# Attention probabilities in a one-core Trainium2 kernel: split into f16 halves in SBUF and turned by transposing transfers

## The chip, the core and the metric

The kernel runs on one core of a Trainium2 chip. The core has five engines that run on their own and meet at semaphores: TensorE (PE, matmuls into PSUM), VectorE (DVE), ScalarE (ACT), GpSimd (POOL, which works in SBUF here) and SyncE (SP, which issues nearly all transfers). Sixteen DMA engines move data between HBM and SBUF and inside SBUF. The metric is the device time of one execution in microseconds.

## What is computed

A block with two branches, a gated delta rule and a sparse latent attention, merged by gates and projected. Only the attention matters here. With T = 1024 tokens, 8 heads, a latent of rank 256, and for each query at most 256 chosen keys:

```python
logits = jnp.einsum('bqhc,bqkc->bqhk', ql, kv).astype(f32)
bias = rel_bias[t5_bucket(t[None, :, None] - sel)]
logits = logits + jnp.moveaxis(bias, -1, 2).astype(f32)
logits = jnp.where(valid[:, :, None, :], logits, -jnp.inf)
p = jax.nn.softmax(logits, axis=-1).astype(kv.dtype)
return jnp.einsum('bqhk,bqkc->bqhc', p, kv)
...
ob = jnp.einsum('bthc,chd->bthd', o_lat, w_uv[l]).reshape(B, T, DSA_W) * jax.nn.silu(zb)
```

The kernel builds keys and values of each head from the latent, computes the logits against all earlier keys, and adds a mask that closes the keys that were not chosen. Its f32 matmuls are three f16 ones: each operand is split into a high half and a low half (the rest), and `three` (L92) adds high x high, high x low and low x high.

## The kernel before

The program has a front (projections and choice of keys), a delta-rule stage, the attention (`phase_attention`, L2325) and a merge (`phase_merge`, L2122). The order on each engine is the order of its code; nothing is scheduled.

The attention walks over 64 steps n = (h, i), eight query tiles i of 128 tokens for each head h, in the order 0, 7, 1, 6, 2, 5, 3, 4 (`ORDER`). A step is `wide[n]` = 128 (i + 1) columns wide, so a head has 36 blocks of 128x128, and narrow and wide steps alternate: 128, 1024, 256, 896, 384, 768, 512, 640. Work on one step is spread over loops that run at different distances:

- PE, loop pass n: logits of step n (L2427), transposes of step n - 3 from SBUF into PSUM (`turn`, L2442), products with the values of step n - 5 (`values`, L2455), and in every second pass a piece of the next head's keys or values (`piece`, L2397).
- ACT, pass n: exp of step n - 1 with its row sums (`soften`, L2495), the high half of a piece (L2486), the high half of the turned probabilities of step n - 3 from PSUM (`split_p`, L2500), the high half of the gated output of step n - 7 (`split_b`, L2508).
- DVE, pass n: reciprocal of the row sums of step n - 2 (`norm`, L2553), logits plus mask with the row extreme for step n - 1 (`peak`, L2542, which reads PSUM and `added`), gate of step n - 6 (`gate`, L2566), low half of the turned probabilities of step n - 4 (`split_p`, L2559), low half of a piece (L2531).
- POOL, pass n: scaling of the probabilities of step n - 2 by the reciprocal (L2614), low half of the gated output of step n - 8 (L2619), mask plus bias for step n + 2 (`near`, L2599). In eight passes it also splits a part of the output weights (L2627).
- SP loads one gate row block of 512 KB per head (L2389).

Probabilities lie in four places of `g.o` (`place`); wide scores have one place in PSUM (banks 0 and 1) and narrow ones another, and the turned blocks use banks 3 to 5. Scores of step n wait until `peak` of step n - 2 is done. In each pass DVE's reciprocal waits for ACT's exp of the same step, ACT's exp for DVE's peak, and DVE's low half of a piece for ACT's high half of it.

## Time and profile before

| | |
|---|---|
| time, median of 3 runs | 1411.44 us (1408.17, 1411.44, 1420.66) |
| span of the profiled execution | 1410.0 us |
| PE busy in the span | 1375.1 us (98%) |
| DVE, ACT, POOL busy | 923.7 us (66%), 716.5 us (51%), 599.8 us (43%) |
| attention stage | about 1063 to 1237 us from the span's start |

The profile is one execution, recorded by the hardware profiler. A timeline row gives the start (us from the span's start), the duration in us, the engine, the line of the kernel, the operation and its tiles as out<-in with partitions x elements; in brackets stands how long the engine sat idle before it and what released it. Instructions on one engine overlap at their ends, so the next one can start a little before the listed end. A group row gives the count, busy us, the mean duration in ns, and idle time with its releaser. Ends of matmuls are modelled; starts are read.

### The profile page before, as it was taken

The numbers are of one execution on the slowest core, as the hardware profiler recorded it, in microseconds if no ns is written. First come the engines' busy times: TensorE is split into PE (matmuls) and PEld (weight loads), VectorE is DVE, ScalarE is ACT, GpSimd is POOL, SyncE is SP. The second block draws the span as 40 slices with busy tenths as digits, with TensorE's granted clock in tenths as the row PEclk, the third lists the DMA queues.
The fourth block names the chain that finished last, engine by engine and source line by source line (L and its number), as shares of the span: only waits on it lengthen the run. The fifth ranks groups of instructions, "written<-read, shape, count | busy, mean of one in ns | idle before, by whom it ended". The sixth has DMA issues, their size and how long they took to land.

```text
span 1410.0 us, 27056 instructions
## 1 busy us (share of the span) xinstructions
PE 1375.1 (98%) x10290; PEld 843.0 (60%) x10298; DVE 923.7 (66%) x1958; ACT 716.5 (51%) x1525; POOL 599.8 (43%) x717
## 2 busy tenths in 40 slices
PE   6999999999999999999999999999999999999997
PEld 6555994444444556666666666554446878844444
DVE  4879887777334577678778775446716777747344
ACT  4758777785433554655665663333215777701111
POOL 0074677778752442541531530003104777764000
PEclk9989999999999999999999999999999999999999
DMA  9401333333323321322222222337652000085122
GB/s 366 140 8 31 93 106 113 120 121 110 108 90 124 84 71 52 87 63 72 82 66 67 83 71 80 122 97 276 199 197 103 31 22 26 17 305 157 38 97 90
DMA packets 137642, 147.50 MB, mean 105 GB/s; under 512 B 16706, under 2 KB 109738, under 8 KB 135852
## 3 DMA queue, kind: packets, MB, share of 16 engines
q1 hardware_dynamic: 136668, 141.31, 31.8%
q10 hardware_dynamic: 720, 4.46, 0.8%
q8 instruction: 81, 1.33, 0.4%
q14 instruction: 45, 0.37, 0.1%
q0 software_dynamic: 128, 0.03, 0.0%
HBM read 114.40 MB, written 31.15 MB: 103 GB/s over the span
## 4 chain that ended last, share of the span: by engine, by line
PE 58%; DVE 3%; POOL 2%; issue 2%; DMA 2%; ACT 2%; SPq 1%; DVEq 0%; POOLq 0%; ACTq 0%
PE ps L94 15%; PE ps L96 15%; PE ps L95 15%; PE ps L2451 2%; DVE g_yq L1632 1%; POOL g_shared L1397 1%; PE ps L1915 1%; PE ps L2039 1%; POOL g_shared L1399 1%; PE ps L2023 1%; PE ps L2022 1%; PE ps L2018 1%; PE ps L2038 1%; PE ps L1953 1%; DMA g_shared<-diagonal_blocks 1%
## 5 line engine op out<-in xcount | busy, mean ns | idle before, releaser
L94 PE MATMUL ps<-g_h_hi,g_piece_hi 128*128 128x512 f16 x544 | 206.9, 380 | 1.6 <-PEq L2662 1.6
L95 PE MATMUL ps<-g_h_lo,g_piece_hi 128*128 128x512 f16 x544 | 206.3, 379 | 0.0
L96 PE MATMUL ps<-g_h_hi,g_piece_lo 128*128 128x512 f16 x544 | 206.2, 379 | 0.0
L1397 POOL TENSOR_TENSOR g_shared<-g_shared 128x120 f32<-128x120 f32 (+14 forms) x120 | 58.0, 483 | 181.7 <-DMA g_shared<-diagonal_blocks 171.3
L1010 DVE TENSOR_SCALAR_CACHE_REDUCE a_ada<-a_ada,a_s_all 128x896 bf16<-128x896 f32 (+1 forms) x124 | 113.0, 967 | 1.0
L1632 DVE SCALAR_TENSOR_TENSOR g_yq<-e_raw,g_taps,g_yq 128x1024 f32<-128x1024 f32 x60 | 92.3, 1539 | 21.5 <-ACT g_yq L1461 19.7
L94 PE MATMUL ps<-g_o,g_h_hi 128*128 128x128 f16 (+2 forms) x424 | 101.4, 266 | 1.7 <-DVE l_b L2572 1.6
L96 PE MATMUL ps<-g_o,g_h_lo 128*128 128x128 f16 (+2 forms) x424 | 101.4, 266 | 0.4
L95 PE MATMUL ps<-g_o,g_h_hi 128*128 128x128 f16 (+2 forms) x416 | 98.3, 264 | 0.0
L96 PEld LDWEIGHTS ps<-g_h_hi,g_piece_lo 128*128 128x128 bf16 x544 | 53.3, 98 | 64.4 <-issue 0.3
L94 PEld LDWEIGHTS ps<-g_h_hi,g_piece_hi 128*128 128x128 f16 x544 | 53.3, 98 | 53.4 <-issue 2.2
L95 PEld LDWEIGHTS ps<-g_h_lo,g_piece_hi 128*128 128x128 f16 x544 | 53.3, 98 | 50.2
L2614 POOL TENSOR_SCALAR g_o<-g_o,l_share 128x128 f32<-128x128 f32 (+3 forms) x64 | 47.9, 748 | 72.3 <-DVE l_share L2557 71.9
L1493 ACT ACTIVATE g_shared<-ps,e_s_neg 128x128 f32<-128x128 f32 x56 | 20.6, 368 | 104.5 <-PE ps L2023 104.2
L1623 DVE TENSOR_TENSOR g_piece_lo<-g_piece,g_piece_hi 128x1024 bf16<-128x1024 f32 x40 | 50.0, 1250 | 30.9 <-ACT g_piece_hi L1544 30.8
L310 POOL TENSOR_TENSOR a_work<-a_w,a_work 128x512 bf16<-128x512 f32 x48 | 56.6, 1195 | 15.3 <-ACT a_work L722 15.3
L310 POOL TENSOR_TENSOR a_parts<-a_w,a_parts 128x512 bf16<-128x512 f32 x48 | 55.1, 1165 | 13.3 <-ACT a_parts L722 13.3
L2497 ACT ACTIVATE g_o<-g_o,l_top 128x128 f32<-128x128 f32 (+3 forms) x64 | 49.7, 776 | 20.6 <-DVE l_top L2550 18.7
L739 ACT ACTIVATE a_ada<-a_ada,a_s_all 128x1024 bf16<-128x1024 f32 (+1 forms) x62 | 57.3, 927 | 0.7 <-DVEq L1032 0.7
L1399 POOL TENSOR_TENSOR g_shared<-g_shared 128x120 f32<-128x120 f32 (+14 forms) x120 | 53.6, 447 | 9.4
L2506 ACT CAST g_o<-ps 128x128 f16<-128x128 f32 (+3 forms) x64 | 40.7, 636 | 26.5 <-PE ps L2451 24.9
L1544 ACT CAST g_piece_hi<-g_piece 128x1024 f16<-128x1024 f32 x40 | 41.6, 1040 | 24.0 <-DMA g_piece<-in_w_o_gdn 22.4
(437 smaller groups left out, 4052.1 us busy)
## 6 DMA issues: line engine op xcount, KB each, us to landing
a_w<-in_w_in SPq DMA_DIRECT2D x17, 1024.0 KB, 5.8
g_piece<-in_w_in SPq DMA_DIRECT2D x34, 512.0 KB, 4.1
channel_gates<-a_ada SPq DMA_DIRECT2D x48, 256.0 KB, 2.2
g_shared<-diagonal_blocks SPq DMA_DIRECT2D x32, 256.0 KB
a_ada<-in_w_ada ACTq DMA_DIRECT2D x4, 1024.0 KB, 9.5
a_x<-in_x SPq DMA_DIRECT2D x8, 512.0 KB, 8.9
delta_gate<-a_ada SPq DMA_DIRECT2D x16, 256.0 KB, 2.5
g_shared<-sums_by_head SPq DMA_DIRECT2D x8, 512.0 KB, 4.3
```

Source lines behind the costliest of these rows:

```text
L94: pe.matmul(out, a_hi, b_hi, start=first, stop=False)
L95: pe.matmul(out, a_hi, b_lo, start=False, stop=False)
L96: return pe.matmul(out, a_lo, b_hi, start=False, stop=last)
L310: nc.gpsimd.tensor_tensor(op_lo[v % 2][:, x], of, op_hi[v % 2][:, x], ALU.subtract).then_inc(w_ready, 1)
L739: nc.scalar.activation(mask[:, g.first[i]:g.first[i + 1]], score[:, g.first[i]:g.first[i + 1]], ACT.Sign, bias=trial[:, 4 + e:5 + e], accu ...
L1010: mark(("count", e), nc.vector.tensor_scalar(spent_of(i), rows_of(i), trial[:, e:e + 1], offset[:, e:e + 1], ALU.is_ge, ALU.add, accum_out ...
L1397: nc.gpsimd.tensor_tensor(part, table[:, j, :, j + 1:BASE], tc[:, :, j:j + 1].broadcast_to([P, NT, left]), ALU.mult).then_inc(sub, 1)
L1399: last = nc.gpsimd.tensor_tensor(tc[:, :, j + 1:BASE], tc[:, :, j + 1:BASE], part, ALU.subtract)
L1623: nc.vector.tensor_tensor(w_lo[:, m % 3], w32[:], w_hi[:, m % 3], ALU.subtract).then_inc(w_ready, 1)
L1632: nc.vector.scalar_tensor_tensor(out=y, in0=raw[:, m % 2, PAD - 3 + j:PAD - 3 + j + T], scalar=g.taps[:, tap:tap + 1], in1=y, op0=ALU.mult ...
L2497: nc.scalar.activation(p(n), p(n), ACT.Exp, scale=-1.0, bias=top[:, n % 4:n % 4 + 1], accum_out=total[:, n % 4:n % 4 + 1]).then_inc(exp_ok, 1)
L2614: nc.gpsimd.tensor_scalar(p(m), p(m), share[:, m % 4:m % 4 + 1], 1.0, ALU.mult, ALU.mult).then_inc(shared, 1)
```

## The change

Five things change in `phase_attention`:

- The transposes on PE, their PSUM banks and the two reads of them (ACT's high half, DVE's low half) are gone. ACT makes the high half straight from the probabilities in SBUF, multiplied by the reciprocal, as f16 (`high`); DVE computes probability x reciprocal - high half with one SCALAR_TENSOR_TENSOR (`low`). Both halves of a step lie side by side in one of four staging buffers, in tiles that the earlier stages used.
- SP issues one transposing transfer a step, SBUF to SBUF, of both halves (2 x `wide[n]` columns). It waits for both halves and, from step 4 on, for the products of step n - 4. `high` of step n waits for the transfer of step n - 4.
- POOL's scaling is gone. POOL takes over the high half of the gated output from ACT, ahead of its low half.
- Wide scores get a second place (bank 3), so their logits wait for the peak of step n - 4. Outputs alternate between banks 5 and 6.
- The distances: `high` and `low` stand in the pass of the reciprocal (n - 2), products at n - 6, gate at n - 7.

```diff
+        staged = lambda n: (rest[:, 2 * T:], wide_a, narrow_b, rest)[n % 4][:, 0:2 * wide[n]]
...
-            return (0 if steps[n][1] >= 4 else 2) * BANK
+            return ((0, 3)[n // 2 % 2] if steps[n][1] >= 4 else 2) * BANK
...
+            for n in range(N):
+                sp.wait_ge(high_ok, n + 1)
+                sp.wait_ge(low_ok, n + 1)
+                if n >= 4:
+                    sp.wait_ge(pv, n - 3)
+                sp.dma_start_transpose(pt(n), staged(n)).then_inc(turned[n % 4], 16)
+                h = n // 8 + 1
+                if n % 8 == 5 and 2 <= h < H:
                     sp.wait_ge(got, NT * (h - 1))
-                sp.dma_start(z[:, h % 2], g.sig_dram[h * P:(h + 1) * P, :]).then_inc(z_in[h % 2], 16)
+                    sp.dma_start(z[:, h % 2], g.sig_dram[h * P:(h + 1) * P, :]).then_inc(z_in[h % 2], 16)
...
-                if n >= 2:
+                if steps[n][1] < 4 and n >= 2:
                     pe.wait_ge(top_ok, n - 1)
-                pe.wait_ge(kv_l, 4 * h + 2)
+                elif n >= 4:
+                    pe.wait_ge(top_ok, n - 3)
+                pe.wait_ge(kv_l, 4 if n == 3 else 4 * h + 2)
...
             def values(n):
                 h, i = steps[n]
-                pe.wait_ge(pt_l, n + 1)
+                pe.wait_ge(turned[n % 4], TURNED_BEFORE + 16 * (n // 4 + 1))
...
+            def high(n):
+                act.wait_ge(inv, n + 1)
                 if n >= 4:
+                    act.wait_ge(turned[n % 4], TURNED_BEFORE + 16 * (n // 4))
+                nc.scalar.activation(staged(n)[:, 0:wide[n]], p(n), ACT.Copy, scale=share[:, n % 4:n % 4 + 1]).then_inc(high_ok, 1)
...
+                if 0 <= n - 2 < N:
+                    high(n - 2)
                 if 0 <= n - 1 < N:
                     soften(n - 1)
                 if piece_of(n - 1) is not None and n != 4:
                     piece(piece_of(n - 1))
-                if 0 <= n - 3 < N:
-                    split_p(n - 3)
-                if 0 <= n - 7 < N:
-                    split_b(n - 7)
...
+            def low(n):
+                dve.wait_ge(high_ok, n + 1)
+                nc.vector.scalar_tensor_tensor(out=staged(n)[:, wide[n]:], in0=p(n), scalar=share[:, n % 4:n % 4 + 1], in1=staged(n)[:, 0:wide[n]],
+                                               op0=ALU.mult, op1=ALU.subtract).then_inc(low_ok, 1)
...
-                if 0 <= n - 6 < N:
-                    gate(n - 6)
-                if 0 <= n - 4 < N:
-                    split_p(n - 4)
+                if 0 <= n - 7 < N:
+                    gate(n - 7)
+                if 0 <= n - 2 < N:
+                    low(n - 2)
...
+                    pool.wait_ge(got, n - 8 + 1)
+                    nc.gpsimd.tensor_copy(q_hi[:, h, i * P:(i + 1) * P], b32[:, (n - 8) % 3]).then_inc(b_h, 1)
                     pool.wait_ge(b_h, n - 8 + 1)
```

DVE's list of instructions, from the reciprocal of a 1024-wide step on, before (L2557 is the reciprocal, L2550 the peak with the read of its extreme, L2572 the gate, L2563 the low half read from PSUM, L2536 the low half of a piece):

```order
1163 L2557 RECIPROCAL l_share<-l_total 128x1
1164 L2550 ISA g_o,l_top<-ps,g_arena 128x256
1165 L2550 ISA l_top 128x1
1166 L2572 TENSOR_TENSOR l_b<-ps,g_o 128x128
1167 L2563 TENSOR_TENSOR g_o<-ps,g_o 128x640
1168 L2557 RECIPROCAL l_share<-l_total 128x1
1169 L2550 ISA g_o,l_top<-ps,g_h_hi 128x896
1170 L2550 ISA l_top 128x1
1171 L2572 TENSOR_TENSOR l_b<-ps,g_o 128x128
1172 L2563 TENSOR_TENSOR g_o<-ps,g_o 128x128
1173 L2536 TENSOR_TENSOR g_h_lo<-ps,g_h_hi 128x512
```

The same place after the change (L2546 reciprocal, L2539 peak, L2559 gate, L2550 the low half, L2526 the piece):

```order
1164 L2546 RECIPROCAL l_share<-l_total 128x1
1165 L2539 ISA g_o,l_top<-ps,g_arena 128x256
1166 L2539 ISA l_top 128x1
1167 L2559 TENSOR_TENSOR l_b<-ps,g_o 128x128
1168 L2550 SCALAR_TENSOR_TENSOR g_piece<-g_o,l_share,g_piece 128x1024
1169 L2546 RECIPROCAL l_share<-l_total 128x1
1170 L2539 ISA g_o,l_top<-ps,g_h_hi 128x896
1171 L2539 ISA l_top 128x1
1172 L2559 TENSOR_TENSOR l_b<-ps,g_o 128x128
1173 L2550 SCALAR_TENSOR_TENSOR g_piece_lo<-g_o,l_share,g_piece_lo 128x256
1174 L2526 TENSOR_TENSOR g_h_lo<-ps,g_h_hi 128x512
```

Between the same reciprocal and peak and the next reciprocal now stands the low half of the step whose reciprocal opens the pass (1024, 256 wide) instead of that of the step two before (640, 128 wide).

ACT's list before, over the same two passes (L2497 exp, L2506 high half read from PSUM, L2511 high half of the gated output, L2490 high half of a piece):

```order
922 L2497 ACTIVATE g_o,l_total<-g_o,l_top 128x1024
923 L2490 CAST g_h_hi<-ps 128x512
924 L2506 CAST g_o<-ps 128x640
925 L2511 CAST g_yq<-l_b 128x128
926 L2497 ACTIVATE g_o,l_total<-g_o,l_top 128x256
927 L2506 CAST g_o<-ps 128x128
928 L2511 CAST g_yq<-l_b 128x128
929 L2497 ACTIVATE g_o,l_total<-g_o,l_top 128x896
930 L2490 CAST g_h_hi<-ps 128x512
```

ACT's list after (L2496 exp, L2503 high half, L2489 piece):

```order
905 L2496 ACTIVATE g_o,l_total<-g_o,l_top 128x1024
906 L2489 CAST g_h_hi<-ps 128x512
907 L2503 ACTIVATE g_piece<-g_o,l_share 128x1024
908 L2496 ACTIVATE g_o,l_total<-g_o,l_top 128x256
909 L2503 ACTIVATE g_piece_lo<-g_o,l_share 128x256
910 L2496 ACTIVATE g_o,l_total<-g_o,l_top 128x896
911 L2489 CAST g_h_hi<-ps 128x512
```

The high half of a step now stands between its own exp and the exp of the next step, and it reads the column that DVE's reciprocal writes.

## Rows read from the trace of the kernel before

**Rows 1.** Windows: stretch, its length, busy us (instructions) by engine, granted clock, DMA.
```profile
1100.00:1120.00 20.00, 20.00 (x224) 16.11 (x222) 15.04 (x43) 14.77 (x35) 16.05 (x27) 1.00 0.04 14
```

**Rows 2.** Chain that ended last, attention: start us, us, what, how many.
```profile
1138.14 0.87 PE ps L2451 x8
...
1159.23 0.87 PE ps L2451 x8
```

**Rows 3.** Timeline of DVE, 1138 to 1160: start us, us, engine, line, operation.
```profile
1138.99 0.15 DVE L2557 RECIPROCAL l_share<-l_total 128x1 f32<-128x1 f32 x1
...
1141.24 0.15 DVE L2557 RECIPROCAL l_share<-l_total 128x1 f32<-128x1 f32 x1
...
1144.43 0.15 DVE L2557 RECIPROCAL l_share<-l_total 128x1 f32<-128x1 f32 x1
...
1146.55 0.15 DVE L2557 RECIPROCAL l_share<-l_total 128x1 f32<-128x1 f32 x1
...
1149.49 0.15 DVE L2557 RECIPROCAL l_share<-l_total 128x1 f32<-128x1 f32 x1
...
1151.24 0.15 DVE L2557 RECIPROCAL l_share<-l_total 128x1 f32<-128x1 f32 x1
...
1151.46 1.23 DVE L2550 CUSTOM_DVE_ANT_0 g_o<-ps,g_h_hi 128x1024 f32<-128x1024 f32 x1
...
1154.47 0.69 DVE L2536 TENSOR_TENSOR g_h_lo<-ps,g_h_hi 128x512 f16<-128x512 f32 x1 [0.98 <-ACT g_h_hi L2490]
...
1155.08 0.15 DVE L2557 RECIPROCAL l_share<-l_total 128x1 f32<-128x1 f32 x1
...
1156.51 0.15 DVE L2557 RECIPROCAL l_share<-l_total 128x1 f32<-128x1 f32 x1
```

**Rows 4.** Timeline of ACT, the copy of a piece inside iteration (1,8).
```profile
1153.88 0.56 ACT L2490 CAST g_h_hi<-ps 128x512 f16<-128x512 f32 x1
```

**Rows 5.** Groups by line and shape, ACT and DVE: count, busy us, mean ns.
```profile
L2497 ACT ACTIVATE g_o<-g_o,l_top 128x1024 f32<-128x1024 f32 x8 | 9.2, 1150 | 1.8 <-DVE l_top L2550 1.4
...
L2497 ACT ACTIVATE g_o<-g_o,l_top 128x512 f32<-128x512 f32 x8 | 5.8, 722 | 1.3 <-DVE l_top L2550 0.6
...
L2255 ACT ACTIVATE g_arena<-g_arena,i_tail 128x512 f32<-128x512 f32 x1 | 0.7, 722 | 0.2 <-DVE i_tail L2315 0.2
...
L2550 DVE CUSTOM_DVE_ANT_0 g_o<-ps,g_h_hi 128x1024 f32<-128x1024 f32 x8 | 9.8, 1225 | 0.4
...
L2550 DVE CUSTOM_DVE_ANT_0 g_o<-ps,g_h_lo 128x640 f32<-128x640 f32 x8 | 6.4, 804 | 0.0
```

**Rows 6.** The same groups, DVE's SCALAR_TENSOR_TENSOR with a column as scalar.
```profile
L2293 DVE SCALAR_TENSOR_TENSOR g_arena<-g_arena,i_ss 128x1024 f32<-128x1024 f32 x7 | 9.0, 1284 | 0.2
...
L1719 DVE SCALAR_TENSOR_TENSOR g_shared<-ps,g_decays,g_arena 128x128 f32<-128x128 f32 x56 | 19.3, 345 | 21.8 <-PE ps L2018 21.8
```

**Rows 7.** Timeline of DVE, end of attention: last reciprocal, last gate.
```profile
1229.17 0.16 DVE L2557 RECIPROCAL l_share<-l_total 128x1 f32<-128x1 f32 x1 [0.32 <-ACT g_o L2497]
...
1235.77 0.29 DVE L2572 TENSOR_TENSOR l_b<-ps,g_o 128x128 f32<-128x128 f32 x1 [1.18 <-PE ps L96]
```

**Rows 8.** DVE and POOL, 1249 to 1256; line L2271; two POOL instructions of attention.
```profile
1250.23 4.07 POOL L2206 TENSOR_TENSOR g_o<-g_shared,g_o 128x2048 bf16<-128x2048 f32 x1
...
1252.24 0.69 DVE L2268 TENSOR_TENSOR g_arena<-ps,g_arena 128x512 f32<-128x512 f32 x1 [16.18 <-DMA g_arena<-channel_gates]
...
1253.01 1.83 DVE L2271 TENSOR_TENSOR g_arena<-g_arena 128x512 f32<-128x512 f32 x1
...
L2271 DVE TENSOR_TENSOR g_arena<-g_arena x16: 691/692/3848, 1253.0 to 1319.7; 128x512 f32<-128x512 f32 x16
...
1156.42 0.43 POOL L2619 TENSOR_TENSOR g_yq<-l_b,g_yq 128x128 f16<-128x128 f32 x1
...
1156.81 0.67 POOL L2605 TENSOR_TENSOR g_h_lo<-g_arena 128x256 f32<-128x256 bf16 x1
```

**Rows 9.** The plain 512 KB loads of L2389: from issue to landing.
```profile
DMA to landing us min/median/max: 3.2/3.4/9.1
```

More of the change, by code:

```diff
@@ L2338, in phase_attention @@
         p = lambda n: flat[:, 0:3 * T][:, place(n)]
-        pt_all = [flat[:, (6 + 3 * n) * BANK:(9 + 3 * n) * BANK].bitcast(F16) for n in range(2)]
-        pt_hi, pt_lo = (lambda n, t=t: t[:, place(n)].rearrange("p (j t) -> p j t", t=P) for t in pt_all)
+        pt_all = flat[:, 3 * T:6 * T].bitcast(F16)
+        both_of = lambda n: slice(2 * place(n).start, 2 * place(n).start + 2 * wide[n])
+        pt = lambda n: pt_all[:, both_of(n)].rearrange("p (j t) -> p j t", t=P)
+        wide_a, rest = g.piece32[:].rearrange("p k n -> p (k n)").bitcast(F16), g.piece_hi[:].rearrange("p u k n -> p (u k n)")
+        narrow_b = g.piece_lo[:].rearrange("p u k n -> p (u k n)").bitcast(F16)
+        staged = lambda n: (rest[:, 2 * T:], wide_a, narrow_b, rest)[n % 4][:, 0:2 * wide[n]]
         z = flat[:, 6 * T:8 * T].rearrange("p (s t) -> p s t", t=T)
@@ L2460, in values @@
                     pe.wait_ge(kv_l, 6)
[L2461 to L2463 removed]
+                elif n >= 2:
+                    pe.wait_ge(got, n - 1)
                 for j in range(i + 1):
[L2465 removed]
+                    last = three(nc.tensor, out_at(n), v_hi[:, h % 2, j], v_lo[:, h % 2, j], pt(n)[:, j], pt(n)[:, i + 1 + j], j == 0, j == i)
                 last.then_inc(pv, 1)
@@ L2469, in _ @@
                 piece(m)
-            for n in range(N + 5):
+            for n in range(N + 6):
                 if n < N:
```

71 lines of the change are left out of this document (16 added, 55 removed).

## The prediction

> **What bounds the kernel now.** I read the windows of the attention stage first. TensorE (PE) is busy all 20.00 us of 20 at a granted clock of 1.00, while DVE has 15.04, ACT 14.77 and POOL 16.05 [rows 1]. The chain that ended last shows the rhythm: the eight f32 transposes of width 1024 open at 1138.14 and again at 1159.23, so a head takes 21.09 us [rows 2]. So PE is full. That alone says that whatever leaves PE is won.
>
> Then I read DVE and ACT as lists in order of time, because their steps wait for each other. Call an iteration (a, b): DVE takes the reciprocal of step a, then the peak of step b, a gate, a split, and every second time the split of a piece of the next head's keys or values. The reciprocals start at 1138.99, 1141.24, 1144.43, 1146.55, 1149.49, 1151.24, 1155.08, 1156.51 [rows 3], and 21.09 later the round starts again. The iterations, by widths of (a, b) in units of 128, are: (7,3) 2.25, (3,6) 3.19, (6,4) 2.12, (4,5) 2.94, (5,1) 1.75, (1,8) 3.84, (8,2) 1.43, (2,7) 3.57. The four with a piece sum to 13.54, the four without to 7.55.
>
> The four with a piece hang on a chain that has no PE in it. For (1,8): peak at 1151.46 for 1.23, a hop of 0.04, exp for 1.15, ACT's copy of the piece from 1153.88 for 0.56, DVE's subtraction from 1154.47, next reciprocal 0.61 later at 1155.08 [rows 3 to 5]. As a formula, reciprocal to peak 0.07, peak P(b), hop 0.04, exp E(b), copy and hop 0.60, subtraction 0.61. With P and E from [rows 5] (0.14 and 0.107 less for each 128 columns less) this gives (1,8) 3.69, (2,7) 3.45, (3,6) 3.20, (4,5) 2.96, together 13.30, against 13.54 measured. So this ring of two engines is nearly as long as PE's work: a second bound stands right behind the first.
>
> **What the change takes from PE.** The transposes: 0.87 for eight [rows 2], 0.109 each, 36 a head, 3.92 us. PE's work for a head falls to 21.09 - 3.92 = 17.2 us. If PE alone set the pace, eight heads would give 31 us back.
>
> **What it does to the ring.** In (a, b) DVE now subtracts for step a, just scaled, and no longer for the step two before it. The low half needs the high half, which ACT makes only after this iteration's reciprocal. So an iteration without a piece becomes: 0.19 from the reciprocal's start to ACT (its 0.15 and a hop of 0.04), high half H(a), hop 0.04, low half L(a), less the 0.08 by which the next DVE instruction overlaps (1154.47 + 0.69 against 1155.08 [rows 3]); H + L + 0.15 in all.
> - H(a): the trace has a Copy with a column as scale, 128x512 in 0.722 [rows 5]; the exp of the same width takes the same 0.722. I take H = E: 1.15, 1.04, 0.94, 0.83 for widths 8, 7, 6, 5. Its lower bound is ACT's plain copy of a piece of 512, 0.56 [rows 4], 0.16 less each.
> - L(a): SCALAR_TENSOR_TENSOR takes 1.284 for 1024 and 0.345 for 128 [rows 6], so 1.28, 1.15, 1.01, 0.88 by interpolation.
> - Sums: (8,2) 2.58, (7,3) 2.34, (6,4) 2.10, (5,1) 1.86, together 8.88 against 7.55. In the iterations with a piece a is narrow, high and low fit beside the peak, the exp and the copy (L(1) is over 1.7 us after the reciprocal, the piece is ready at 3.1), and PE's small delays leave: 13.30 against 13.54.
> - A full head: 13.30 + 8.88 = 22.18, 1.09 more than now. PE with 17.2 no longer matters, and its savings end as idle time.
>
> **Head by head.** Seven heads with pieces of the next: 7 x 1.09 = 7.6 us. In the last head no pieces stand; its iterations become H + L + 0.15 or, where the exp ends last, 0.24 + P(b) + E(b) (the 0.24 are 0.07, 0.04, the 0.09 by which the exp's sum is read late, and a hop): 2.62, 2.58, 2.37, 2.34, 2.12, 2.10, 1.88 = 16.0. Now the same seven take 1229.17 less the reciprocal of (1,8) three heads after 1151.24, 1214.5, so 14.7 [rows 3, 7]: +1.3. The tail from the last reciprocal to the last gate, 6.6 us now [rows 7], loses scaling on POOL, five transposes and two PSUM reads, and gets 1.02 for H with its start, 0.88 for L, about 3.4 for the transfer (a plain 512 KB one lands in 3.4 [rows 9]) and the same products of about 1.0: 6.4, -0.2. Together +8.7 us.
>
> **The low half beside GpSimd.** L reads both inputs from SBUF; every DVE instruction of this stage so far had PSUM as one of them, or only one input. What that means is seen at 1253.01: a DVE product of two SBUF tiles takes 1.83; the 16 of its line have 0.692 as the median; this one ends 0.54 after a POOL instruction that ran from 1250.23 for 4.07. The product just ahead, with PSUM as one input, takes its 0.69 beside the same POOL instruction [rows 8]. So such an instruction waits until POOL's current one is over. In this stage POOL now starts its work on b32 about 0.1 after the gate: copy (about as long as the low half), low half 0.43, then the bias of 256 columns 0.67 [rows 8]. The gate ends at 0.28 + P(b) after the reciprocal, L wants to start at 0.23 + H(a). For (8,2) POOL is busy from 0.8 to 2.3 and L comes at 1.38; for (7,3) 0.9 to 2.4 and 1.27; for (6,4) 1.1 to 2.5 and 1.17; for (5,1) 0.65 to 2.1 and 1.06. All four meet a running instruction, with rests of 0.2, 0.0 to 0.4, 0.3, 0.4. I take 0.9 us a head, 7 in all. Bounds: nothing, and a whole 0.67 each time, 2.7 a head, 22 in all. In piece iterations the wait has cover.
> The Trainium skill (SBUF — State Buffer, Who interferes with whom) says the same of a two-input VectorE instruction against a GpSimd one that reads SBUF, but as an exclusive lock held by whichever starts first; by that GpSimd's own instructions also wait behind each low half, which here has slack, since POOL loses its scaling. Without the lock the sum would be 1420, with it 1427.
>
> **The transfers.** 64 of them; a head moves 4608 columns in two halves, 2304 KB, 4.5 times the 512 KB that land plainly in 3.2 to 9.1 us, 3.4 in the middle [rows 9]. One after another that is 15.3 us of a head of 22 or more. The four staging buffers are the first to feel a late one: the high half of step n + 4 waits for the transfer of step n, three whole iterations after its low half, 3.45 + 2.34 + 3.20 = 9.0 us for width 8 (512 KB). PE's values come four iterations after the low half. So I cost them at nothing outside the tail; cover ends near 9 us for a wide one, or, by rate, at 22 / 72 = 0.31 us for one block of 128x128. SP's queue holds behind a waiting transfer only the gate load of the next head, needed ten iterations on.
> The Trainium skill speaks both ways. Advanced Engine Details and Errata (X-Bar Transpose) has such transfers as fast as ordinary ones. VectorE: DVE Perf Modes (The three transpose paths) gives 1309 ns for one 128x128 block; taken as a rate, an estimate of 94 us a head. No row here shows a transposing transfer.
>
> **Sum.** The profiled span is 1410.0; the runs' median is 1411.4, 1.4 above. 1410.0 + 8.7 + 7 + 1.4 = 1427 us.
>
> **Rivals.**
> - The ring without contention: 1410.0 + 8.7 + 1.4 = 1420. For it: POOL may drift so that its instructions lie elsewhere. 0.26.
> - PE sets the pace and the gain lands: 1411 - 31 = 1380, or part of it. For it: PE has no idle time now. Against: the measured iterations with a piece have no PE in them and already take 13.5 of 21.1; it needs H + L + 0.15 over the four others to stay under 7.8, that is each pair 0.3 shorter than the rows say, before anything is won. 0.06.
> - The transfers are slower than their cover: at 9.1 us for 512 KB, the worst landing in [rows 9], a head needs 41 us, 20 more than now: 1411 + 8 x 20 = 1571. It decides from 0.31 us a block. For it: nothing but a late landing among plain loads; against: the other landings. 0.08. The Trainium skill's 1309 ns a block (VectorE: DVE Perf Modes, The three transpose paths) would be this case, and worse.
> - The forecast, ring with contention of 0.4 to 2.7 us a head, 1423 to 1441: 0.60.
>
> **Numbers.** Likeliest 1427. The range 1415 to 1442 takes the ring with none and with full contention and the cheaper H (four times 0.16 a head, -5); it leaves out the two rivals of 0.06 and 0.08. A measurement of this kernel can tell about 1% (14 us) from no change. Slower by over 1% (above 1425.6): three quarters of 0.60, a tenth of 0.26, and 0.08, together 0.56. Within 1%: 0.38. Faster: 0.06.
>
> **What would show it.** In the new trace: a head 22.2 to 24 us long, by the reciprocals; DVE idle just before the low half with ACT's high half as releaser; low halves of width 1024 longer than 1.28 on the mean; PE with gaps in every head, its wait on the peak or the transfer; 17 us of PE work a head; transfers landing well under 9 us; ACT's high half 1.15 for 1024. Wrong: heads under 21 us (then H or L overlap more than I see), POOL or DMA as the engine waited for, low halves at 1.28 flat (no contention, 1420), or wide transfers above 9 us, with ACT waiting for them at the high half.

## The result, and the profile after

| | before | after |
|---|---|---|
| median of the runs compared, 4 and 4 | 1409.81 us | 1426.09 us |
| ratio after/before, 95% interval | | 1.0115, 1.0065 to 1.0164 |
| span of the profiled execution | 1410.0 us | 1426.1 us |
| start of the stage: first reciprocal of attention | 1068.20 | 1071.23 |
| the stage: first reciprocal to last gate | 167.57 | 180.56 |
| from the last gate to the end | 174.2 | 174.3 |

The changed kernel is slower by 1.15%, 16.3 us between the medians. In the two traces 13.0 us of that lie in the attention. The merge behind it is unchanged. The remaining 3.0 us lie ahead of the attention; they are taken up below.

The first view to read is again the window of the stage, in the columns of [rows 1]:

```profile
1100.00:1120.00 20.00, 15.88 (x184) 11.42 (x183) 15.48 (x42) 13.05 (x26) 14.15 (x24) 1.00 0.82 146
```

PE did its work: it is busy 15.88 us of 20 where it was busy all 20, at the same granted clock of 1.00. GpSimd (POOL) and ACT have less to do as well. No engine is full any more, and yet the stage is longer. That is the picture of a ring: engines that wait for one another in turn.

DVE in order of time shows the ring, where [rows 3] showed it before (start, duration, then line and operation, in brackets idle time and its releaser). L2546 is the reciprocal, L2550 the new low half, L2526 the low half of a piece:

```profile
1138.30 0.15 DVE L2546 RECIPROCAL l_share<-l_total 128x1 f32<-128x1 f32 x1
...
1141.36 0.69 DVE L2526 TENSOR_TENSOR g_h_lo<-ps,g_h_hi 128x512 f16<-128x512 f32 x1 [1.13 <-ACT g_h_hi L2489]
1141.97 0.15 DVE L2546 RECIPROCAL l_share<-l_total 128x1 f32<-128x1 f32 x1
...
1143.34 1.28 DVE L2550 SCALAR_TENSOR_TENSOR g_piece<-g_o,l_share,g_piece 128x1024 f16<-128x1024 f32 x1 [0.69 <-ACT g_piece L2503]
1144.54 0.16 DVE L2546 RECIPROCAL l_share<-l_total 128x1 f32<-128x1 f32 x1
...
1147.97 0.15 DVE L2546 RECIPROCAL l_share<-l_total 128x1 f32<-128x1 f32 x1
...
1149.24 1.37 DVE L2550 SCALAR_TENSOR_TENSOR g_piece_hi<-g_o,l_share,g_piece_hi 128x896 f16<-128x896 f32 x1 [0.44 <-ACT g_piece_hi L2503]
1150.53 0.15 DVE L2546 RECIPROCAL l_share<-l_total 128x1 f32<-128x1 f32 x1
```

The iteration (8,2), from 1141.97 to 1144.54, takes 2.57 us where it took 1.43. Inside it DVE sits idle for 0.69 us with ACT's high half as the releaser, and then makes the low half for 1.28. The iteration (1,8) ahead of it takes 3.67 and still hangs on the piece (1.13 idle, released by ACT's copy). From the second to the seventh head, five are 22.48 or 22.49 us long and one 22.74, against 20.99 to 21.10 before.

The lengths of the new operations, as groups by shape over the stage (count, busy us, mean ns, idle before), answer to [rows 5, 6]:

```profile
L2503 ACT ACTIVATE g_piece<-g_o,l_share 128x1024 f16<-128x1024 f32 x8 | 9.2, 1150 | 6.0 <-DVE l_share L2546 6.0
...
L2550 DVE SCALAR_TENSOR_TENSOR g_piece<-g_o,l_share,g_piece 128x1024 f16<-128x1024 f32 x8 | 10.4, 1300 | 5.5 <-ACT g_piece L2503 5.5
L2550 DVE SCALAR_TENSOR_TENSOR g_piece_hi<-g_o,l_share,g_piece_hi 128x896 f16<-128x896 f32 x8 | 10.5, 1314 | 3.5 <-ACT g_piece_hi L2503 3.5
L2550 DVE SCALAR_TENSOR_TENSOR g_piece_hi<-g_o,l_share,g_piece_hi 128x640 f16<-128x640 f32 x8 | 8.2, 1021 | 4.1 <-ACT g_piece_hi L2503 4.1
```

ACT's scaled copy is as long as the exp of its width. The low half of 896 columns is on the mean longer than that of 1024, so something other than its width lengthens it. The transfers, last, answer to [rows 9]; these lines say who waited for them in the whole run (us, times; L94 is the first of the three products, PEld its weight load) and how long they took from issue to landing:

```profile
  PEld ps L94: 5.3, 4
  PE ps L94: 1.5, 1
...
DMA to landing us min/median/max: 2.3/4.0/6.5
```

### The profile page after: what moved, and what is told of

It reads as the page before. It is cut to its first block, busy times and chain, and to the rows that moved or that the text cites. A ratio compares the mean times of both kernels' runs of the same rounds, so it can differ in the third digit from the quotient of the medians.

```text
span 1426.1 us, 26485 instructions
## 1 busy us (share of the span) xinstructions
PE 1356.2 (95%) x10010; PEld 813.3 (57%) x10010; DVE 935.4 (66%) x1958; ACT 711.6 (50%) x1461; POOL 603.5 (42%) x717
## 3 DMA queue, kind: packets, MB, share of 16 engines
q8 instruction: 78, 1.28, 0.4%
## 4 chain that ended last, share of the span: by engine, by line
PE 47%; issue 6%; DVE 5%; ACT 5%; POOL 3%; DMA 2%; SPq 1%; DVEq 0%; POOLq 0%; ACTq 0%
PE ps L94 12%; PE ps L95 12%; PE ps L96 12%; DVE g_o L2539 2%; DVE g_yq L1632 1%; ACT g_piece L2503 1%; POOL g_shared L1397 1%; PE ps L1915 1%; ACT g_piece_hi L2503 1%; PE ps L2039 1%; POOL g_shared L1399 1%; PE ps L2023 1%; PE ps L2022 1%; PE ps L2018 1%; PE ps L2038 1%
## 5 line engine op out<-in xcount | busy, mean ns | idle before, releaser
L94 PE MATMUL ps<-g_h_hi,g_piece_hi 128*128 128x512 f16 x544 | 206.6, 380 | 1.6 <-PEq L2646 1.6
L94 PE MATMUL ps<-g_o,g_h_hi 128*128 128x128 f16 (+2 forms) x424 | 102.6, 268 | 13.3 <-DVE l_b L2559 11.4
L95 PE MATMUL ps<-g_o,g_h_hi 128*128 128x128 f16 (+2 forms) x424 | 102.7, 269 | 0.0
L94 PEld LDWEIGHTS ps<-g_h_hi,g_piece_hi 128*128 128x128 f16 x544 | 53.3, 98 | 53.3 <-issue 2.0
L1623 DVE TENSOR_TENSOR g_piece_lo<-g_piece,g_piece_hi 128x1024 bf16<-128x1024 f32 x40 | 50.0, 1250 | 31.1 <-ACT g_piece_hi L1544 30.9
L94 PEld LDWEIGHTS ps<-g_o,g_h_hi 128*128 128x128 f16 x424 | 41.9, 99 | 37.5 <-issue 19.4
L310 POOL TENSOR_TENSOR a_parts<-a_w,a_parts 128x512 bf16<-128x512 f32 x48 | 55.1, 1163 | 13.3 <-ACT a_parts L722 13.3
L2496 ACT ACTIVATE g_o<-g_o,l_top 128x128 f32<-128x128 f32 (+3 forms) x64 | 49.1, 768 | 12.8 <-DVE l_top L2539 12.7
L94 PE MATMUL ps<-g_arena 128*128 128x128 f16 (+1 forms) x160 | 34.6, 253 | 21.9 <-DVE g_h_lo L2526 13.7
```

The costliest lines, as they stand in the source:

```text
L94: pe.matmul(out, a_hi, b_hi, start=first, stop=False)
L95: pe.matmul(out, a_hi, b_lo, start=False, stop=False)
L310: nc.gpsimd.tensor_tensor(op_lo[v % 2][:, x], of, op_hi[v % 2][:, x], ALU.subtract).then_inc(w_ready, 1)
L1623: nc.vector.tensor_tensor(w_lo[:, m % 3], w32[:], w_hi[:, m % 3], ALU.subtract).then_inc(w_ready, 1)
L2496: nc.scalar.activation(p(n), p(n), ACT.Exp, scale=-1.0, bias=top[:, n % 4:n % 4 + 1], accum_out=total[:, n % 4:n % 4 + 1]).then_inc(exp_ok, 1)
```

## The experiments

The runs are compared by two numbers. The time and its ratio to the kernel before come from several executions on the same chip, but they also carry what the rest of the program does. The lengths in the trace (a head, the last seven iterations, the tail, the stage) come from one execution each and are far steadier: before, the last five full heads agree within 0.01 us. In the fastest variants they are less steady: up to the last head, three of the kernels below have the same order of instructions, and their heads are 18.77, 18.63 and 19.14.

| kernel | time | before beside it | ratio (95%) | head | last seven | tail | stage |
|---|---|---|---|---|---|---|---|
| before | | | | 21.09 | 14.65 | 6.60 | 167.6 |
| after | 1426.1 | 1409.8 | 1.0115 (1.0065 to 1.0164) | 22.54 | 16.18 | 7.11 | 180.6 |
| before, one block turned | 1401.4 | 1407.8 | 0.9942 (0.9909 to 0.9976) | 19.64 | 14.47 | 6.29 | 158.8 |
| before, piece later | 1407.2 | 1412.0 | 0.998 (0.9947 to 1.0012) | 21.09 | 14.49 | 6.59 | 166.4 |
| after, more PE work | 1428.5 | 1407.8 | 1.013 (1.0079 to 1.018) | 22.53 | 16.18 | 9.30 | 182.7 |
| after, half the bytes | 1423.3 | 1407.8 | 1.011 (1.0051 to 1.0169) | 22.53 | 16.18 | 5.66 | 179.1 |
| after, light GpSimd | 1423.0 | 1407.8 | 1.0107 (1.007 to 1.0145) | 22.45 | 15.99 | 6.51 | 179.2 |
| after, piece later | 1399.6 | 1412.0 | 0.9944 (0.9891 to 0.9997) | 19.31 | 16.17 | 6.45 | 158.2 |
| the same again | 1402.0 | 1408.0 | 0.9959 (0.9929 to 0.9989) | 19.23 | 16.19 | 6.77 | 157.9 |
| after, low half later | 1412.2 | 1412.0 | 1.0024 (0.999 to 1.0058) | 21.02 | 15.52 | 8.23 | 170.7 |
| after, both later | 1399.1 | 1412.0 | 0.9907 (0.9867 to 0.9948) | 18.77 | 16.84 | 8.13 | 155.0 |
| the same again | 1398.2 | 1407.9 | 0.9927 (0.9894 to 0.996) | 18.63 | 15.77 | 8.20 | 155.1 |
| after, wide low half later | 1403.2 | 1408.0 | 0.9954 (0.992 to 0.9988) | 19.47 | 17.10 | 7.61 | 160.6 |
| after, both later but in the last head | 1395.4 | 1407.9 | 0.9906 (0.9866 to 0.9945) | 19.14 | 16.35 | 6.97 | 155.9 |

"Head" is the mean of the third to seventh head, by the reciprocals that open them; "last seven" runs from the reciprocal of the first step of the last head to that of its last step, "tail" from there to the start of the last gate.

**What PE's transposes were worth.** In the kernel before, only one block of each step is turned:

```diff
-                for j in range(i + 1):
+                for j in range(i + 1 if h == 0 else 1):
                     last = nc.tensor.transpose(g.ps[:, at + j * P:at + (j + 1) * P], p(n)[:, j * P:(j + 1) * P],
```

> The kernel before, with one transposed block of 128x128 in a step instead of wide[n]/128, from the second head on (the first head is whole). It leaves out part of the computation: the probabilities of the other blocks are stale. Everything else, with both reads of PSUM, stands. PE's work falls by 28 blocks of 0.109 us in a head, 3.05 us, so by 21 us over seven heads. Theory (a ring of DVE and ACT stands right behind PE): the ring's iterations are 13.3 us with a piece and, without PE, reciprocal to reciprocal about 0.24 + P(b) + E(b) or the sum of DVE's own work, about 7.4 us, together 20.7: a head shrinks by 0.4 us or less, the time by under 4 us, and PE shows idle time in each head. Rival (PE alone sets the pace): a head falls from 21.1 to about 18.1 us, the time by about 21 us, to 1390.

A head fell to 19.64 us: neither the 18.1 of PE as the only bound nor the 20.7 that was expected of the ring. The ring stands right behind PE, but 1.45 us behind, not 0.4. The timeline of DVE shows both kinds of its iterations:

```profile
1149.12 0.69 DVE L2536 TENSOR_TENSOR g_h_lo<-ps,g_h_hi 128x512 f16<-128x512 f32 x1 [0.98 <-ACT g_h_hi L2490]
1149.73 0.15 DVE L2557 RECIPROCAL l_share<-l_total 128x1 f32<-128x1 f32 x1
...
1151.06 0.15 DVE L2557 RECIPROCAL l_share<-l_total 128x1 f32<-128x1 f32 x1
...
1153.89 0.69 DVE L2536 TENSOR_TENSOR g_h_lo<-ps,g_h_hi 128x512 f16<-128x512 f32 x1 [1.27 <-ACT g_h_hi L2490]
1154.49 0.15 DVE L2557 RECIPROCAL l_share<-l_total 128x1 f32<-128x1 f32 x1
```

(8,2), from 1149.73 to 1151.06, is 1.33 and full of DVE's own work; (2,7) is 3.43 with a wait for the piece. The four iterations with a piece sum to 13.24, the others to 6.40 (1.33, 1.87, 1.87, 1.33). The expectation had put 7.4 for the latter, about what the full kernel shows, where PE holds them up. So of the 3.05 us taken from PE's head here, 1.45 arrive.

**Whether the ring also paces the kernel before.** DVE's low half of a piece is moved one pass later, ahead of the pass's other low half, so that it no longer stands behind ACT's exp and copy:

```diff
-                if n == 4:
-                    piece(5)
...
+                if piece_of(n - 2) is not None:
+                    piece(piece_of(n - 2))
                 if 0 <= n - 4 < N:
                     split_p(n - 4)
-                if piece_of(n - 1) is not None and n != 4:
-                    piece(piece_of(n - 1))
```

> The same move of the piece's low half in the kernel before. Theory (PE, with its transposes, sets the pace of 21.1 us there and the ring of 19.6 us stands behind it): a head stays at 21.1 us within 0.2, the time within 4 us of before, 1404 to 1412. Rival (the ring of DVE and ACT also sets the pace before, since four of its iterations have no PE in them): a head falls by more than 0.5 us, the time by more than 4 us.

The head is 21.09 us to the hundredth, though its iterations inside changed (2.59, 2.68, 2.35, 3.46, 2.11, 3.21, 1.87, 2.82 from (1,8) on). From the second head on PE alone paces the kernel before, and a shorter ring brings it nothing. Only the first head fell, from 19.86 to 18.76, and the last seven iterations by 0.16.

**Whether PE is waited for after the change.** About 4 us of PE work a head are put back, as products that are overwritten:

```diff
+                for _ in range((1, 1, 2, 3, 3, 4, 5, 5)[i]):
+                    three(nc.tensor, out_at(n), v_hi[:, h % 2, 0], v_lo[:, h % 2, 0], pt(n)[:, 0], pt(n)[:, i + 1], True, True)
                 for j in range(i + 1):
```

> The kernel after, with 24 more groups of three products a head on PE in the products with the values (block 0 again, into the same output, which the real first product then opens anew, so nothing of the result changes): about 4 us of PE work a head, what the change had taken away, now again inside PE's pass. Theory (the ring of DVE and ACT sets the pace and PE has about 5 us of slack a head): the head stays at 22.7 us within 0.4, the time within 5 us of the kernel after, 1426 to 1432. Rival (PE sets the pace in the kernel after): the head grows by up to 4 us, the time by up to 32 us, to about 1455.

```profile
1100.00:1120.00 20.00, 19.41 (x248) 15.48 (x249) 15.88 (x41) 12.99 (x25) 15.29 (x24) 1.00 0.65 123
```

PE is busy 19.41 us of 20 instead of 15.88, and the head stays at 22.53 us against 22.54. All of the work that the change took from PE can be put back without a cost, except in the tail (9.30 against 7.11), where nothing covers it. The theory held, the rival fell.

**Whether the transfers are waited for.**

```diff
+                some = wide[n] * (2 if n < NT else 1)
-                sp.dma_start_transpose(pt(n), staged(n)).then_inc(turned[n % 4], 16)
+                sp.dma_start_transpose(pt(n)[:, 0:some // P], staged(n)[:, 0:some]).then_inc(turned[n % 4], 16)
```

> The kernel after, with SP's transposing transfer moving only the high half of the probabilities from the second head on, half the bytes; the low half of the turned ones is stale, so part of the computation is left out. Theory (the transfers lie under their cover): a head stays at 22.7 us within 0.2; the time changes only by the last transfer, 0 to -1.5 us, so 1424 to 1426. Rival (the transfers hold ACT, PE, or the port of the SBUF): with half the bytes a head falls by more than 0.5 us, the time by more than 4 us.

The head is 22.53 us with half the bytes, though the landing fell with them (median 2.9 us instead of 4.0). Only the tail falls, by 1.45 us. So the transfers were covered in the heads, and neither their bytes nor their landing belongs to the 13 us; the last one does belong to the tail.

**What GpSimd adds.** The edit cuts its three operations to 4 columns from the second head on (the bias and the two halves of the gated output), here for one of them:

```diff
-                    nc.gpsimd.tensor_copy(q_hi[:, h, i * P:(i + 1) * P], b32[:, (n - 8) % 3]).then_inc(b_h, 1)
+                    cut = P if n - 8 < NT else 4
+                    nc.gpsimd.tensor_copy(q_hi[:, h, i * P:i * P + cut], b32[:, (n - 8) % 3, :cut]).then_inc(b_h, 1)
```

> The kernel after, with GpSimd's work of the attention cut from the second head on: the bias, the high half and the low half of the gated output are each made for 4 columns only, so part of the computation is left out (those values are stale). The instructions and their order stand, their durations fall to a small part. Theory (an instruction of DVE with two SBUF inputs waits behind GpSimd's running one, 0.56 us a head): the low half of width 1024 falls from a mean of 1300 ns to 1.28, that of 896 from 1314 to 1.15, 640 and 512 from 1021 and 983 to 0.88 and about 0.75; a head falls from 22.7 to about 22.2 us, the time by about 4 us, to 1422. Rival (the low half costs what it costs without GpSimd): the means and the 22.7 us stay. Rival (GpSimd itself is waited for): a head falls by more than 1 us.

The mean over the heads moved by only 0.09 us, less than expected, and the low halves of 1024 columns became longer on the mean, 1332 ns instead of 1300, where 1280 had been expected; those of 896 fell to 1248, not to 1150. Taken alone this would speak for the first rival. Head by head it does not. GpSimd also splits the output weights in eight passes, which this kernel left in place. In the fourth head that split met a low half with cover, and there the iterations (7,3) and (5,1) are 2.37 and 1.84, where the kernel after has 2.56 and 1.99 to 2.02; that head is 22.17 us long, and the seventh 22.13. In the heads of 22.5 to 22.7 the weights' split met a low half without cover. Timeline of DVE in the fourth head, low halves of 896 and 640:

```profile
1153.87 1.18 DVE L2550 SCALAR_TENSOR_TENSOR g_piece_hi<-g_o,l_share,g_piece_hi 128x896 f16<-128x896 f32 x1 [0.44 <-ACT g_piece_hi L2503]
...
1164.29 0.88 DVE L2550 SCALAR_TENSOR_TENSOR g_piece_hi<-g_o,l_share,g_piece_hi 128x640 f16<-128x640 f32 x1 [0.50 <-ACT g_piece_hi L2503]
```

And one head later, DVE and POOL in the timeline, the low half beside the split of the weights on POOL (L2613, L2615):

```profile
1176.03 1.58 DVE L2550 SCALAR_TENSOR_TENSOR g_piece_hi<-g_o,l_share,g_piece_hi 128x896 f16<-128x896 f32 x1 [0.44 <-ACT g_piece_hi L2503]
...
1176.06 0.61 POOL L2613 CAST g_shared<-g_shared 128x512 f16<-128x512 f32 x1
1176.75 1.88 POOL L2615 TENSOR_TENSOR g_shared<-g_shared 128x512 bf16<-128x512 f32 x1
```

The low half took 1.58 instead of 1.18; POOL's subtraction behind the copy, 1.16 when alone, took 1.88. Each was lengthened once. The low half even starts 0.03 us ahead of the copy by the record, and it is still the low half that becomes longer, so the recorded order of two starts this close does not tell which one gets its way. GpSimd's share of a head is 22.49 - 22.13 = 0.36 us, and it goes by which instructions meet.

**The cure: the piece later.** The same edit as above, now in the kernel after:

```diff
-                if n == 4:
-                    piece(5)
...
+                if piece_of(n - 2) is not None:
+                    piece(piece_of(n - 2))
                 if 0 <= n - 2 < N:
                     low(n - 2)
-                if piece_of(n - 1) is not None and n != 4:
-                    piece(piece_of(n - 1))
```

> The kernel after, with DVE's low half of a piece one pass later, ahead of the pass's own low half, so that it no longer stands between ACT's exp and copy and the next reciprocal. Theory (the ring of DVE and ACT is the bound, and its iterations with a piece wait for peak, exp, copy and subtraction in a row): without that wait an iteration is the longer of 0.24 + P(b) + E(b) and DVE's and ACT's own work; by the rows this gives (1,8) 2.62, (8,2) 2.72, (2,7) 2.37, (7,3) 2.48, (3,6) 2.12, (6,4) 2.24, (4,5) 1.88, (5,1) 2.0, together 18.4 us, some 19 with GpSimd's share, instead of 22.5. Seven heads shorten by 3.5 to 4.1 us: 1424 - 27 = about 1397, under the kernel before. PE, with 17.2 us of work, is then close. Rival (the pieces' PSUM place becomes late: PE's next piece waits for the later subtraction): a head stays above 20.5 us, the time above 1408.

```profile
1144.42 1.15 ACT L2503 ACTIVATE g_piece<-g_o,l_share 128x1024 f16<-128x1024 f32 x1
...
1144.84 0.68 DVE L2526 TENSOR_TENSOR g_h_lo<-ps,g_h_hi 128x512 f16<-128x512 f32 x1
1145.60 1.29 DVE L2550 SCALAR_TENSOR_TENSOR g_piece<-g_o,l_share,g_piece 128x1024 f16<-128x1024 f32 x1
```

One instruction of every second pass, in another place, takes 3.2 us off each head (22.54 to 19.31) and turns 1.2% slower into 0.5% faster. In the rows, the piece's low half now fills the time in which DVE waited for ACT's high half: ACT makes it from 1144.42 to 1145.57, and the low half starts at 1145.60, 0.03 us behind it and 0.08 us after the piece's low half ends. The expected iterations were 2.62, 2.72, 2.37, 2.48, 2.12, 2.24, 1.88, 2.0; measured, over five heads, 2.59, 2.81, 2.35, 2.65, 2.11, 2.71, 1.94, 2.14. The sum is 19.3, above the bare 18.4. Most of the difference is an error of the expectation: it let (8,2), (7,3) and (6,4) fall by 0.24 each time, but as the low half becomes shorter the peak becomes longer, and the two together take 1.70, 1.71 and 1.71 us in the rows of this run (0.42 + 1.28, 0.56 + 1.15, 0.69 + 1.02). With 2.72 for all three the sum would have been 19.15. DVE is now busy about 18 of 20 us (17.3 to 18.7 by window), so a low half that meets GpSimd has less cover. The second run of the same kernel says the same:

> The same kernel as in the run with the piece's low half one pass later, to narrow its interval. Theory: the stage is 158 us again, 9 under that of before, so the ratio is 0.9935 within 0.003. Rival (the first result was the clock of those runs): the ratio is 1 within 0.003.

The ratio is 0.9959 with an upper end of 0.9989, the stage 157.9 us. The interval of each of the two runs lies below 1, and the heads show the same gain in both. The stage is 9.4 and 9.6 us shorter than before; the medians say 12.4 and 6.0, which shows how much coarser they are.

**The low half later.**

```diff
-                if 0 <= n - 2 < N:
-                    low(n - 2)
+                if 0 <= n - 3 < N:
+                    low(n - 3)
```

> The kernel after, with DVE's low half of a step one pass later (n - 3), so that it no longer waits for ACT's high half of the same pass. Theory (the low half's wait for the high half makes the iterations without a piece H + L + 0.15): these become about 1.9, 1.9, 1.9, 1.5 = 7.1 us instead of 9.2, the ones with a piece stay at 13.3; a head is 20.4 us, about 2 less, the time 1424 - 17 = 1407. Rival (the transfer, issued one pass later while the products stay where they are, lands too late for PE: it has two passes, about 5 us, and a 512 KB one landed in up to 6.5 us): PE waits for it and a head stays near 22 us or above.

The iterations without a piece came out as worked out: 1.86, 1.86, 1.86, 1.43, together 7.0 against 7.1. Those with a piece did not stay at 13.3 but took 14.0 (3.83, 3.66, 3.35, 3.17), so the head is 21.02, not 20.4. The timeline of DVE shows why:

```profile
1146.17 0.16 DVE L2546 RECIPROCAL l_share<-l_total 128x1 f32<-128x1 f32 x1
1146.38 1.23 DVE L2539 CUSTOM_DVE_ANT_0 g_o<-ps,g_h_hi 128x1024 f32<-128x1024 f32 x1
```

The peak starts 0.21 us after the reciprocal's start, where it starts 0.07 after it in the rows of the kernel after. In this run the 0.21 stands in all four iterations with a piece, and there DVE had a gap ahead of the reciprocal (0.13 us in the row above, 0.22 to 0.92 with ACT's exp as the releaser in the others); where there is none it stays at 0.07. Why a gap has this effect no run here shows. Four times 0.14 is 0.56 of the 0.7 us. The tail grew to 8.23, for the last transfers are issued a pass later. The rival did not set the head either: PE waited for transfers in the whole stage, 17.6 us in weight loads (24 times) and 9.9 us in products (16 times), but the iterations without a piece came out as if it had not.

**Both.**

> The kernel after, with both moves: the piece's low half and the probabilities' low half one pass later each. Theory (ring): no iteration waits for a chain any more; by the rows a head is 17.1 to 17.5 us, where PE's 17.2 us is met, so the time would be about 1424 - 7 x 5.2 = 1388. Rival (the transfer lands too late: two passes are now only 4.3 us, and 512 KB landed in 4.0 to 6.5 us): PE waits for the transfer in the wide steps, one to two us each, a head is 18.5 to 21 us, the time 1395 to 1412.

The head is 18.77 us and the time 1399. Both lie in the rival's range (18.5 to 21, 1395 to 1412), near its lower end, and outside the theory's. Here the transfers do cost something, in the lines on who waited for them (us, times):

```profile
  PEld ps L94: 14.8, 14
  PE ps L94: 9.9, 7
  ACT g_piece_lo L2503: 6.6, 6
  ACT g_piece_hi L2503: 3.5, 3
  ACT g_piece L2503: 2.8, 3
```

ACT, which never waited for a transfer in the kernel after, waits 12.9 us. So the cover that the prediction counted on is real and finite: with about 9 us of it nothing was seen, and with one pass less and shorter passes, about 4 to 5 us by the iterations, it ends. At the same time PE reads 19.77 busy of 20 in a window of this run, so three bounds have come within a few per cent of each other. The second run of this kernel:

> The kernel with both moves again, for a narrower interval and beside the one before it. Theory: stage 155 us, 12 to 13 less than before, ratio 0.991 within 0.003, and again ACT and PE that wait for transfers. Rival (the first result was those runs' clock): ratio over 0.996.

Ratio 0.9927, heads of 18.63, stage 155.1: as before.

**Two attempts to do better.** The first delays only the wide low halves, the second drops the delay in the last head:

```diff
+                for m in (n - 3, n - 2):
+                    if 0 <= m < N and n - m == (3 if steps[m][1] >= 4 and m < N - 1 else 2):
+                        low(m)
```

> The kernel after with the piece's low half one pass later, and the probabilities' low half one pass later for wide steps alone (but the last step); the low halves of narrow steps stay. Theory (ring): the wide low half no longer waits for the high half of its own pass, and its transfer is issued about 1 us earlier than with both moves, since the pass of a narrow step is short and the low half of the narrow step no longer stands ahead. Without the transfers as a bound a head is 17.5 to 18.5 us, the last seven iterations under 15.5, the stage 152 to 155 us, the time 1393 to 1397 beside a kernel before at 1411. Rival (two passes of cover stay too short): ACT and PE wait for the transfers over 0.8 us a head as with both moves, a head stays at 18.8 us, the stage at 155, the time at 1397 to 1400.

This failed, and transfers are not enough to explain it: ACT waited for them only 4.5 us instead of 12.9 and PE 17.7 instead of 24.7, and yet a head took 19.47 instead of 18.77. All of DVE's low halves now fall into the passes of narrow steps, where DVE becomes full, while in the others it waits for the exp:

```profile
1150.27 0.16 DVE L2546 RECIPROCAL l_share<-l_total 128x1 f32<-128x1 f32 x1 [0.57 <-ACT g_o L2496]
...
1151.70 1.28 DVE L2550 SCALAR_TENSOR_TENSOR g_piece<-g_o,l_share,g_piece 128x1024 f16<-128x1024 f32 x1
1152.89 0.51 DVE L2550 SCALAR_TENSOR_TENSOR g_piece_lo<-g_o,l_share,g_piece_lo 128x256 f16<-128x256 f32 x1
1153.33 0.15 DVE L2546 RECIPROCAL l_share<-l_total 128x1 f32<-128x1 f32 x1
```

The expectation had added up the work of two passes; the ring takes the longer engine in each pass.

```diff
+                for m in (n - 3, n - 2):
+                    if 0 <= m < N and n - m == (3 if m < N - NT else 2):
+                        low(m)
```

> The kernel with both moves, but in the last head (which has no pieces) the probabilities' low half is back in its own pass. Theory (the two moves pay only where a piece or a wait for the high half stands in the ring; in the end the low half's later pass and a late transfer only lengthen the tail): the last seven iterations and the tail are 16.2 + 6.5 = 22.7 us as with the piece's move alone, instead of 16.8 + 8.1 = 24.9; a head before it stays at 18.8 us; the stage is 153 us, 2 less than with both moves, the time about 1395 beside 1408, ratio 0.990. Rival (the clock and the transfers decide the end, not the order): the last seven and the tail stay at 24.9 within 0.7.

The last seven and the tail came to 23.3 us, near the expected 22.7 and under the 24.0 and 25.0 of the two runs with both moves everywhere. But in this trace the heads were 19.14 on the mean, not 18.8, with the same instructions in the same order, so the stage was 155.9 and not the expected 153; the cause stays open. The time, 1395.4, is the lowest of all; its interval (0.9866 to 0.9945) overlaps that of both moves everywhere, so between those two nothing is settled. Against the kernel before each of the two is faster, this one by 0.9%.

## Why the prediction came out

The time was forecast as 1427 and is 1426.1. The mechanism was the right one; the sum is less exact than that looks. Step by step:

- **PE sets the pace before, and a ring of DVE and ACT stands behind it.** Right: a shorter ring changed nothing before, and taking the transposes away uncovered a ring of 19.64 us.
- **PE's work falls to 17.2 us a head and no longer matters.** Right: 15.88 of 20 us busy is 17.9 for a head of 22.5, and 4 us a head could be put back for nothing.
- **Iterations with a piece, 13.30.** Measured 3.67, 3.43, 3.18, 2.95, together 13.23. The formula took 0.07 from reciprocal to peak, and its own rows show 0.22 for (1,8) (1151.24 to 1151.46); that is the 0.15 by which (1,8) was measured longer than worked out before the change. After it, that step is 0.07 or 0.08 in 58 of 63 iterations.
- **Iterations without, H + L + 0.15, together 8.88.** Where GpSimd stayed out of the way (the fourth head of the run with light GpSimd) they are 2.57, 2.37, 2.10 and 1.84, together 8.88. H = E held in every width (1150 ns for 1024).
- **GpSimd, 0.9 us a head.** The term was too large: 0.36. All four low halves do meet a running instruction, as forecast, with 0.18, 0.42, 0.15 and 0.33 to 0.37 us of it left (forecast: 0.2, 0.0 to 0.4, 0.3, 0.4). The step that failed is "such an instruction waits until POOL's current one is over". The wait ends about 0.20 us before the recorded end of POOL's instruction, so in these heads the low halves of 1024 and 768 columns are not lengthened, that of 896 by 0.22 and that of 640 by 0.14 to 0.17. Timeline of POOL and DVE in the fourth head, beside the low halves of 1143.34 and 1149.24 above:

```profile
1143.09 0.43 POOL L2605 TENSOR_TENSOR g_yq<-l_b,g_yq 128x128 f16<-128x128 f32 x1
1143.47 1.68 POOL L2592 TENSOR_TENSOR g_h_lo<-g_arena 128x256 f32<-128x256 bf16 x1
...
1149.23 0.43 POOL L2605 TENSOR_TENSOR g_yq<-l_b,g_yq 128x128 f16<-128x128 f32 x1
1149.62 1.52 POOL L2592 TENSOR_TENSOR g_h_hi<-g_arena 128x256 f32<-128x256 bf16 x1
...
1154.74 0.29 POOL L2603 CAST g_yq<-l_b 128x128 f16<-128x128 f32 x1 [1.18 <-DVE l_b L2559]
1154.88 1.02 DVE L2550 SCALAR_TENSOR_TENSOR g_piece<-g_o,l_share,g_piece 128x768 f16<-128x768 f32 x1 [0.21 <-ACT g_piece L2503]
...
1159.76 0.67 POOL L2592 TENSOR_TENSOR g_arena<-g_arena 128x256 f32<-128x256 bf16 x1
1160.10 1.02 DVE L2550 SCALAR_TENSOR_TENSOR g_piece_hi<-g_o,l_share,g_piece_hi 128x640 f16<-128x640 f32 x1 [0.50 <-ACT g_piece_hi L2503]
```

  The same holds for all 64 low halves of this trace: the 23 that are longer than alone by 0.05 us or more are so by what is left of POOL's instruction less 0.18 to 0.22 us. The row that the rule was taken from [rows 8] fits it too: the product ends 0.54 after POOL's instruction where it takes 0.69 alone, so its wait ended 0.15 ahead of POOL's end. In the other direction the bias, 0.67 when alone [rows 8], took 1.68: it starts 0.13 after the low half and ends 0.53 after it. So both engines wait, as by the rule that was weighed (the Trainium skill, SBUF — State Buffer, Who interferes with whom): whichever of the two starts first holds the port and the other waits. The traces agree but for starts within 0.03 us of each other. Of the two, GpSimd had the slack. With the measured term the sum would have been 1410.0 + 8.7 + 8 x 0.36 + 1.4 = 1423.
- **Seven heads at +1.09 each.** Six were 22.5 to 22.7 against 21.0 to 21.1, as worked out with GpSimd's share. The first was not: 22.11 against 19.86. Before the change this head was paced by the ring and not by PE: with the piece later in the kernel before, it alone fell (to 18.76). So nearly all of what the ring gained in length showed there, 2.25. The prediction took the steady head for all seven and missed 0.8 us (2.25 less 1.09 and 0.36).
- **The last seven, 16.0.** Measured 16.18, against 14.65.
- **The tail, 6.4, that is -0.2.** Measured 7.11, +0.5. The term for the transfer failed. It was taken from plain loads at 3.4 us; the chain of waits through the tail shows 4.00 for 640 columns in two halves:

```profile
1245.74 0.91 DVE g_piece_hi L2550
1246.65 0.02 SPq L2397
1246.67 0.03 issue
1246.70 4.00 DMA g_o<-g_piece_hi
```

- **Transfers cost nothing outside the tail.** Right, by half the bytes with no change. Their landing, 2.3 to 6.5 us with a median of 4.0, lies under the cover of 9. One block of 128x128 at 1309 ns (the Trainium skill, VectorE: DVE Perf Modes, The three transpose paths) is no rate for a stream of them: the last transfer turned ten blocks in 4.00 us, 0.40 a block, its latency included.
- **The sum.** The stage was forecast to grow by 15.7 us and grew by 13.0: GpSimd 2.9 instead of 7 (-4.1), the first head +0.8, the tail +0.7. What made up for it is the 3.0 us ahead of the attention, where the change moves no instruction. That the forecast came within 1 us of the median is luck: an overshoot of 2.7 us in the stage met 3.0 us that nobody had forecast, and the four runs themselves spread from 1418 to 1433. The window of the first 100 us of before:

```profile
0.00:100.00 100.00, 84.54 (x521) 57.01 (x522) 69.06 (x105) 56.80 (x94) 22.73 (x22) 0.96 0.51 181
```

And of after:

```profile
0.00:100.00 100.00, 84.06 (x510) 57.43 (x511) 66.76 (x102) 55.25 (x91) 21.09 (x19) 0.94 0.51 181
```

  The granted clock is 0.96 and 0.94, and 0.97 and 0.96 in the next hundred. Over the traces of all kernels here the first reciprocal of the attention comes between 1061.2 and 1076.1 us, in no order of the changes (1076.1 is a variant of before, 1075.8 one of after). It goes with the granted clock of these first 200 us: the three earliest starts (1061.2, 1062.3, 1063.3) have 1.00 in both windows, the two latest 0.94 and 0.87. So these 3 us are no part of the change as far as the traces tell. Whether a small part of them is, since the medians also differ by 16 us, stays open: the interval of the ratio, 9 to 23 us, holds the 13 of the stage.

The forecast had put contention at 0.4 to 2.7 us a head, and the 0.36 measured lies just under that, between it and the rival of the ring without contention, which would have given 1420. One of that rival's signs was even seen: the low halves of 1024 columns are 1.28 to 1.29 us in all seven heads with pieces, and their mean of 1.30 comes from the last head (1.41). The contention showed at 896 and 640. PE as the bound and slow transfers were both refuted.

## What to carry to other kernels

Before work is taken off a full engine, lay out the rounds of the engines behind it: what each waits for in one round. Here that ring was 19.64 us behind a PE of 21.09, so taking 3.9 us off PE could bring 1.45 at most, and the way in which it was done (a high half and a low half in one round, one waiting for the other) lengthened the ring to 22.1, and 22.5 with GpSimd. The cure was not less work but another place for one instruction, into the gap that the new wait had opened; in a full head it was worth nothing before the change and 3.2 us after it.

When two engines contend for a port, work out for each meeting who comes first, how much of its instruction is left and which of the two has slack. Here it cost only where the engine on the critical ring came second with over 0.2 us of the other's instruction left.
